# V projected with x as the stationary operand, and a plain fp32 beginning by halves, in a two-layer attention trunk on one core

## The chip, the cores and the metric

The kernel runs on one core of one Trainium2 chip. The metric is the device time of one execution in microseconds (us). The kernel before has a median of 774.34 us over 3 runs (774.07 to 775.7).

A core has a matrix engine (TensorE, PE in the profile; its weight loads are PEld), a vector engine (VectorE, DVE), an activation engine (ScalarE, ACT), a general engine (GpSimd, POOL) and SyncE (SP), which here issues nearly all transfers from memory. The engines run apart and wait for each other by semaphores.

## What is computed

The reference is a trunk of two layers on x of 256 tokens by 1024 columns, fp32. Layer A uses stick-breaking attention, layer B dilated window attention; both are followed by a SwiGLU. The change touches only the first part of layer A, which is this (cut to what matters):

```python
def rms_norm(x, g):
    y = xf * lax.rsqrt(jnp.mean(xf * xf, axis=-1, keepdims=True) + RMS_EPS)
    return (y * g).astype(x.dtype)

def mixer_a(xn, w_qkv, w_o):
    qkv = (xn @ w_qkv).reshape(b, s, 3, N_HEADS, HEAD_DIM)      # 16 heads of 64
    o = stick_breaking_attention(q, k, v)
    return o.reshape(b, s, D_MODEL) @ w_o

# stick_breaking_attention, strict: s < t
z = einsum('qd,kd->qk', q, k) * scale
log_stay = where(strict, log_sigmoid(-z), 0.0)
log_a = log_sigmoid(z) + cumsum(after, reverse=True)
a = where(strict, exp(log_a), 0.0)
out = einsum('qk,kd->qd', a, v)
```

## The kernel before, in words

**Products in high and low parts.** Weights and activations are cut into a high part (fp32r) and a low part, the rest. A product is three matmuls: high by high, high by low, low by high. Weights come in units: SyncE loads a unit into one of 3 places of `raw`, ScalarE makes the high part (`hi`, L476), VectorE the low part (`lo`, L758), each into one of 6 places. In layer A a unit is 128 x 1024 (1024 rows by 128 columns of q, k or v: one pair of heads); from the output weights on it is 128 x 2048. A place of `raw` is free again when its unit's low part is made, and SyncE waits for that before it loads (L306).

**Layer A.** The 16 heads go in 8 pairs. For pair p TensorE projects q, k and v (`project_a`, 24 matmuls each of 256 moving columns: the weights are the stationary operand, x the moving one). The result stands with columns on partitions, which is right for q and k, but V has to be turned: VectorE copies it out with the norm's row factor (`take_v_a`, L886), TensorE turns it by two transposes (`turn_v`, L1214), ScalarE copies it to `va` (L552).

The order of TensorE in a step p: scores of pair p-1 (L1205, L1206), outputs of pair p-2 (L1238, L1240), turning of pair p-1, q, k and the first 6 matmuls of v of pair p, the running sums of pair p-1 (L1227), the other 18 of v. Between scores and sums lies this chain: ScalarE takes absolute value, exponential and logarithm (L544, L546, L548), VectorE makes the softplus and its mask (L858, L860), `arg` (L861), ScalarE the high part (L554), VectorE the low part (L863). After the sums VectorE subtracts them (`stay_a`, L870), ScalarE takes the exponential (L557), VectorE masks (L875). In between stand the cuts of the units of weights. The order of every engine is written out by hand.

**After the last pair** come the output product (`out_proj`, L1150 to L1152, in slices k of the 1024 rows, 512 moving columns) mixed with the last outputs and sums, then the boundary to the SwiGLU.

**The beginning.** SyncE loads the unit matrix `eye`, x in two tiles of 128 tokens (512 KB each), the first query weights by halves, the key and value weights of pair 0, and small things. TensorE runs some matmuls on zeros (`keep_busy`), turns x (16 transposes), and projects. ScalarE and VectorE make the high and low parts of the turned x with its gain (`cut_both`) and of the first two units by halves.

## Time and profile before

| | |
|---|---|
| median of 3 runs | 774.34 us |
| the profiled execution | 774.78 us |
| its span, from first to last instruction | 772.9 us |
| TensorE busy | 763.6 us, 99% |
| VectorE busy | 506.8 us, 66% |
| ScalarE busy | 398.8 us, 52% |
| transfers | 139.17 MB, mean 180 GB/s |

Times inside the program are microseconds from the start of the span. Matmuls overlap, so the distance between the starts of two rows says more than the duration of one. Plain fp32 matmuls are recorded as two passes each. In the timeline, a bracket at the end tells how long the engine was idle before and whom it waited for.

### The profile page before, as it was taken

The page shows a single profiled execution, that of the slowest core. Times are in us where ns is not written, and L with a number is a line of the kernel's source. Part 1 is how long each engine was busy: PE and PEld are TensorE (multiplying, and loading weights), DVE is VectorE, ACT ScalarE, POOL GpSimd, SP SyncE. Part 2 cuts the span into 40 slices and gives each one's busy share as a digit, 9 for nine tenths or more (in the row PEclk, how much of TensorE's full clock was granted, in tenths as well). Part 3 has the DMA queues.
Part 4 walks back from the last instruction along what each step waited for, and adds up shares of the span by engine and source line. Part 5 has one row for each costly group of instructions (what it writes and reads, how often), then busy time and mean ns, then how long its engine had stood idle before and what let it go on. Part 6 is the DMA issues. An engine that isn't in the chain of part 4 may idle for free.

```text
span 772.9 us, 12842 instructions
## 1 busy us (share of the span) xinstructions
PE 763.6 (99%) x4533; PEld 657.7 (85%) x4533; DVE 506.8 (66%) x688; ACT 398.8 (52%) x542; POOL 113.6 (15%) x173
## 2 busy tenths in 40 slices
PE   8999999999999999999999999999999999999996
PEld 7999987878888888999898898898888888888885
DVE  6788987766545545868768668567647755554543
ACT  5665676454334344756666566656545534433421
POOL 2000001520000000215225235144002000000000
PEclk9999999999999999999999999999999999999999
DMA  7534866686665454569775685685643856556502
GB/s 232 163 114 141 234 214 226 199 240 218 204 210 183 163 189 137 145 158 220 189 214 147 164 224 142 163 234 178 215 136 92 290 193 199 179 188 215 193 0 54
DMA packets 161538, 139.17 MB, mean 180 GB/s; under 512 B 6617, under 2 KB 151105, under 8 KB 161505
## 3 DMA queue, kind: packets, MB, share of 16 engines
q1 hardware_dynamic: 157536, 131.55, 55.2%
q0 software_dynamic: 3712, 6.88, 4.9%
q8 instruction: 20, 0.33, 0.2%
q10 hardware_dynamic: 256, 0.30, 0.1%
q14 instruction: 14, 0.11, 0.0%
HBM read 137.60 MB, written 1.11 MB: 179 GB/s over the span
## 4 chain that ended last, share of the span: by engine, by line
PE 93%; DMA 2%; DVE 2%; ACT 1%; issue 1%; SPq 0%; DVEq 0%; POOLq 0%; POOL 0%; ACTq 0%
PE ps L1150 19%; PE ps L1152 19%; PE ps L1151 19%; PE ps L1384 10%; PE ps L1386 5%; PE ps L1156 4%; PE ps L1157 4%; PE ps L1158 4%; DMA raw<-in_w_gate_up 2%; PE ps L1442 1%; DVE w_lo L758 1%; PE ps L1298 1%; PE ps L1412 1%; PE ps L1451 1%; PE ps L1227 1%; ACT w_hi L476 1%
## 5 line engine op out<-in xcount | busy, mean ns | idle before, releaser
L758 DVE TENSOR_TENSOR w_lo<-raw,w_hi 128x2048 fp32r<-128x2048 f32 (+2 forms) x144 | 279.2, 1954 | 48.4 <-ACT w_hi L476 47.1
L476 ACT ACTIVATE w_hi<-raw 128x2048 fp32r<-128x2048 f32 (+2 forms) x144 | 232.7, 1637 | 60.6 <-DMA raw<-in_w_kv_b 22.9
L1150 PE MATMUL ps<-w_hi,xt 128*128 128x512 f32 x352 | 139.5, 396 | 0.0
L1152 PE MATMUL ps<-w_hi,xt 128*128 128x512 f32 x352 | 137.3, 390 | 0.0
L1151 PE MATMUL ps<-w_lo,xt 128*128 128x512 f32 x352 | 137.1, 389 | 0.0
L637 ACT ACTIVATE work<-ps,stat 128x256 f32<-128x256 f32 x44 | 20.9, 476 | 191.8 <-PE ps L1152 191.8
L1150 PE MATMUL ps<-w_hi,ot 128*128 128x512 f32 x240 | 95.0, 396 | 0.7 <-DVE ot L1011 0.4
L1152 PE MATMUL ps<-w_hi,ot 128*128 128x512 f32 x240 | 93.5, 390 | 0.0
L1151 PE MATMUL ps<-w_lo,ot 128*128 128x512 f32 x240 | 93.5, 390 | 0.0
L1152 PEld LDWEIGHTS ps<-w_hi,xt 128*128 128x128 f32 x352 | 66.1, 188 | 14.0
L1150 PEld LDWEIGHTS ps<-w_hi,xt 128*128 128x128 f32 x352 | 66.1, 188 | 13.6 <-issue 0.6
L1151 PEld LDWEIGHTS ps<-w_lo,xt 128*128 128x128 f32 x352 | 66.2, 188 | 12.8
L1009 DVE CAST ot<-ps 128x512 fp32r<-128x512 f32 x22 | 15.2, 691 | 75.5 <-PE ps L1298 75.5
L389 POOL TENSOR_SCALAR stat<-stat 128x1 f32<-128x1 f32 x16 | 10.3, 644 | 366.1 <-ACT work L492 343.2
L1156 PE MATMUL ps<-xt,w_hi 128*128 128x256 f32 x216 | 62.0, 287 | 0.8 <-DVE w_lo L1050 0.8
L1157 PE MATMUL ps<-xt,w_hi 128*128 128x256 f32 x216 | 61.1, 283 | 0.0
L1158 PE MATMUL ps<-xt,w_lo 128*128 128x256 f32 x216 | 61.0, 283 | 0.0
L1150 PEld LDWEIGHTS ps<-w_hi,ot 128*128 128x128 f32 x240 | 45.1, 188 | 11.1 <-DVE w_lo L758 1.0
L1152 PEld LDWEIGHTS ps<-w_hi,ot 128*128 128x128 f32 x240 | 45.0, 188 | 9.6
L1151 PEld LDWEIGHTS ps<-w_lo,ot 128*128 128x128 f32 x240 | 45.1, 188 | 8.9
L429 POOL TENSOR_TENSOR work<-mask_b,work 128x512 f32<-128x512 bf16 x16 | 24.6, 1537 | 137.4 <-DVE stat L939 95.7
L1156 PEld LDWEIGHTS ps<-xt,w_hi 128*128 128x128 f32 x216 | 41.3, 191 | 2.2 <-DVE w_lo L1050 1.4
(143 smaller groups left out, 1211.9 us busy)
## 6 DMA issues: line engine op xcount, KB each, us to landing
raw<-in_w_gate_up SPq DMA_DIRECT2D x88, 512.0 KB, 4.8
raw<-in_w_kv_b SPq DMA_DIRECT2D x96, 256.0 KB, 3.9
raw<-in_w_down SPq DMA_DIRECT2D x22, 1024.0 KB, 4.9
raw<-in_w_q_b SPq DMA_DIRECT2D x48, 256.0 KB, 4.0
raw<-in_w_qkv_a SPq DMA_DIRECT2D x23, 512.0 KB, 4.7
raw<-in_w_o_a SPq DMA_DIRECT2D x4, 1024.0 KB, 7.4
work<-bias_rows POOLq DMA_DIRECT2D x64, 64.0 KB, 3.7
raw<-in_w_o_b SPq DMA_DIRECT2D x4, 1024.0 KB, 6.0
```

The lines of the kernel that those rows point to most:

```text
L429: pool.tensor_tensor(ends[0], ends[1], turned_band, ALU.add)
L476: act.activation(w_hi[:, s % CUT, 0:size(s)], raw[:, s % RAW, 0:size(s)], ACT.Copy).then_inc(hi_made, 1)
L637: act.activation(silu[:, t, :], bank(4 + t, 0, FC), ACT.Silu, scale=x_rs(2 * l + 1, t)).then_inc(silu_made, 1)
L758: dve.tensor_tensor(w_lo[:, c, 0:n], raw[:, s % RAW, 0:n], w_hi[:, c, 0:n].bitcast(F32), ALU.subtract).then_inc(lo_made, 1)
L1150: mm(out, xs[0], ws[0], start=start, stop=False)
L1151: mm(out, xs[0], ws[1], start=False, stop=False)
L1152: return mm(out, xs[1], ws[0], start=False, stop=stop)
L1156: mm(out, ws[0], xs[0], start=start, stop=False)
L1157: mm(out, ws[0], xs[1], start=False, stop=False)
L1158: return mm(out, ws[1], xs[0], start=False, stop=stop)
L1384: mm(both, w[k // 4][0][:, k % 4, g, :], x_[:, :, k, :], start=k == 0, stop=False, skip_group_check=True)
L1386: inst = mm(bank(b, 0, SEQ), w[k // 4][1][:, k % 4, g, :], x_[:, 0, k, :], start=False, stop=k == KT - 1, skip_group_check=True)
```

## The change

**V.** The x is now the stationary operand and the weights the moving one. The result has tokens on partitions, as the outputs need it; no V copy on VectorE and no transposes. One V unit is half of the 1024 rows by 256 columns, that is two pairs of heads; units 2h and 2h+1 give V for pairs 2h and 2h+1. `values_a(h)` has 24 matmuls of 256 columns. Units of pair 0 and 1 come in the beginning, and step p projects V unit p+1 behind the sums, so the last step has none. ScalarE copies both pairs' V to `va` with the row factor, at every second pair.

**The beginning.** x and the first query weights are loaded by halves in turn: the first 512 columns of both token tiles, the first half of the query weights, then the second halves. Each half is turned, copied with its gain to `xf` (plain fp32, ScalarE and VectorE one bank each), and multiplied by the plain fp32 weights, without cuts, 8 matmuls for q and 8 for k. The high and low parts of x are made from `xf` for what follows. The diagonal of row factors is made by VectorE and no more by GpSimd. `eye` is loaded from ScalarE's queue. Because the first q and k need no cut units, the units' numbers shift by two (`A0 = -2`). The mask is loaded after step 1, and x is loaded a second time behind the output weights.

```diff
-A0 = 0
+A0 = -2
...
+        def query_a(p):
+            return A0 + (3 * p + 1 if p else 0)
+        def value_a(h):
+            return A0 + (3 * h if h else 2)
...
+                elif s >= 1:
+                    sp.wait_ge(first_used, s)
...
-            sp.dma_start(eye[:, :], square[:, 0, :]).then_inc(eye_in, 16)
-            for t in range(NT):
-                sp.dma_start(xn[:, t, :], x_dram[t]).then_inc(x_in[t], 16)
-            first = raw[:, 0, 0:KT * P].rearrange("p (k n) -> p k n", k=KT)
-            sp.dma_start(first[:, 0:4], qkv_dram[:, 0, 0:4, 0:P]).then_inc(first_in, 16)
-            sp.dma_start(first[:, 4:8], qkv_dram[:, 0, 4:8, 0:P]).then_inc(landed[0], 16)
-            pair_a(0, 0, (1, 2))
+            for half in range(2):
+                k4, cols = slice(4 * half, 4 * half + 4), slice(HALF * half, HALF * half + HALF)
+                for t in range(NT):
+                    sp.dma_start(xn[:, t, cols], x_dram[t][:, cols]).then_inc(x_in[t][half], 16)
+                sp.dma_start(first_w[0][:, k4], qkv_dram[:, 0, k4, 0:P]).then_inc(first_in[half], 16)
+            sp.dma_start(first_w[1], qkv_dram[:, 1, :, 0:P]).then_inc(first_in[2], 16)
+            half_values_a(0, 0)
...
+            half_values_a(1, 0)
+            step_a(1, 0)
             sp.dma_start(mask_in, mask).then_inc(mask_in_s, 16)
...
+            query_key_a(PAIRS - 1, 0)
+            for u in range(4):
+                two_rows(WOA0 + u, 0, wo_dram[0][:, 2 * u:2 * u + 2, :])
             sp.wait_ge(xt_done, 4)
             sp.wait_ge(xsq_made, NT)
             for r in range(R):
                 sp.dma_start(xn[RUN * (r % 2):RUN * (r % 2) + RUN, r // 2, :], by_residue(x[0])[r]).then_inc(x_again, 16)
...
-                act.wait_ge(vt_done, j * 2 + a + 1)
-                if a >= 1:
-                    act.wait_ge(pva_done, j * 2 + a)
-                act.activation(va, bank(2, 0, SEQ), ACT.Copy).then_inc(va_made, 1)
+                if a % 2 == 0:
+                    act.wait_ge(w_used, j * 6 + value_a(a + 1) + 1)
+                    act.wait_ge(*((pva_done, j * 2 + a) if a else (xrs_made, NT)))
+                    for t in range(NT):
+                        inst = act.activation(va[:, t, :], bank(2, 2 * P * t, 2 * P), ACT.Copy, scale=x_rs(0, t))
+                    inst.then_inc(va_made, 1)
...
+            for half in range(2):
+                turned_x(2 * half)
+                act.wait_ge(xf_act, half + 1)
+                act.wait_ge(xf_dve, half + 1)
+                ks = slice(4 * half, 4 * half + 4)
+                act.activation(xt[:, 0, ks, :], xf[:, ks, :], ACT.Copy).then_inc(xt_hi, 4 * NT)
...
             dve.wait_ge(gain_made, 1)
...
+            turned_x(1)
+            square_first(0)
+            square_first(1)
+            turned_x(3)
...
+            def first_columns(c, ks=range(KT)):
+                for k in ks:
+                    if c == 0:
+                        if k % 2 == 0:
+                            pe.wait_ge(xf_dve if k % 4 else xf_act, k // 4 + 1)
+                        if k % 4 == 0:
+                            pe.wait_ge(first_in[k // 4], 16)
+                    elif k == 0:
+                        pe.wait_ge(first_in[2], 16)
+                    inst = mm(bank(0, SEQ * c, SEQ), first_w[c][:, k, :], xf[:, k, :], start=k == 0, stop=k == KT - 1)
...
-            def turn_v(a, j):
...
+            def values_a(h, j, ks=range(4)):
+                s, half = value_a(h), h % 2
+                pe.wait_ge(lo_made, j * 6 + s + 1)
...
+                w = cut_unit(s, k=4)
+                for k in ks:
+                    for t in range(NT):
+                        out, xs = bank(2, 2 * P * t, 2 * P), [xt[:, n, 4 * half + k, P * t:P * t + P] for n in range(2)]
+                        mm(out, xs[0], w[0][:, k, :], start=not half and k == 0 and t == 0, stop=False,
+                           skip_group_check=True)
+                        mm(out, xs[0], w[1][:, k, :], start=False, stop=False, skip_group_check=True)
+                        inst = mm(out, xs[1], w[0][:, k, :], start=False, stop=half == 1 and k == 3, skip_group_check=True)
...
-                turn_v(p - 1, j)
                 project_a(p, j, 0, 0, 0)
                 project_a(p, j, 1, 0, SEQ)
-                project_a(p, j, 2, 1, 0, range(2))
                 sums_a(p - 1, j)
-                project_a(p, j, 2, 1, 0, range(2, KT))
+                values_a(p + 1, j)
...
-            keep_busy(5)
+            keep_busy(3)
...
+            for half in range(2):
+                ks = range(4 * half, 4 * half + 4)
+                for t in range(NT):
+                    pe.wait_ge(x_in[t][half], 16)
+                    for k in ks:
+                        inst = pe.transpose(bank(4 + k // 2, SEQ * (k % 2) + P * t, P), xn[:, t, P * k:P * k + P],
+                                            eye[:, :])
...
+                keep_busy(1)
+                first_columns(0, ks)
+            first_columns(1)
             pe.wait_ge(ones_in, 16)
             spread_rows(1)
...
+            values_a(0, 0)
+            values_a(1, 0)
```

TensorE at the very beginning, before: L1487 is the matmul on zeros, L1498 the transposes of x, L1156 to L1158 the three matmuls of a product.

```order
1 L1487 MATMUL ps<-rows 128x256 [waits zeros_made]
2 L1487 MATMUL ps<-rows 128x256 x4
3 L1494 MATMUL ps<-eye,work 128x72 [waits gain_in,eye_in]
4 L1498 MATMUL ps<-eye,xn 128x128 [waits x_in0]
5 L1498 MATMUL ps<-eye,xn 128x128 x7
6 L1498 MATMUL ps<-eye,xn 128x128 [waits x_in1]
7 L1498 MATMUL ps<-eye,xn 128x128 x7
8 L1487 MATMUL ps<-rows 128x256 x4
9 L1156 MATMUL ps<-xt,w_hi 128x256 [waits xt_made,first_lo]
```

TensorE at the same place in the changed kernel: L1509 is the matmul on zeros, L1522 a transpose of x, L1207 a plain fp32 matmul of the first q and k.

```order
2 L1509 MATMUL ps<-rows 128x256 x2
3 L1516 MATMUL ps<-eye,work 128x72 [waits gain_in,eye_in]
4 L1522 MATMUL ps<-eye,xn 128x128 [waits x_in00]
6 L1522 MATMUL ps<-eye,xn 128x128 [waits x_in10]
8 L1509 MATMUL ps<-rows 128x256
9 L1207 MATMUL ps<-work,raw 128x256 [waits first_in0,xf_act]
11 L1207 MATMUL ps<-work,raw 128x256 [waits xf_dve]
13 L1522 MATMUL ps<-eye,xn 128x128 [waits x_in01]
17 L1509 MATMUL ps<-rows 128x256
18 L1207 MATMUL ps<-work,raw 128x256 [waits first_in1,xf_act]
20 L1207 MATMUL ps<-work,raw 128x256 [waits xf_dve]
22 L1207 MATMUL ps<-work,raw 128x256 [waits first_in2]
```

The second half's transposes stand behind the first four products, and four of the nine matmuls on zeros are gone.

VectorE in the last two pairs, before: L858 to L863 are the softplus chain of pair 6, L879 and L880 take q and k of pair 7, L886 takes V, L870 subtracts the sums, L758 makes the low part of a unit.

```order
106 L863 TENSOR_TENSOR xkv<-work,xkv 128x768 [waits spl_hi]
107 L879 SCALAR_TENSOR_TENSOR work<-ps,rows 128x256 [waits w_used]
108 L880 TENSOR_TENSOR work<-ps,rows 128x256
109 L758 TENSOR_TENSOR w_lo<-raw,w_hi 128x2048 [waits hi_made]
110 L886 TENSOR_TENSOR work<-ps,rows 128x256 [waits vt_done,w_used]
111 L870 TENSOR_TENSOR work<-work,ps 128x2x256 [waits r_done,arg_made]
113 L758 TENSOR_TENSOR w_lo<-raw,w_hi 128x2048 [waits hi_made]
114 L875 TENSOR_TENSOR work<-work 128x2x2x128 [waits wts_made]
115 L858 SCALAR_TENSOR_TENSOR work<-ps,work 128x768 [waits ell_made]
```

VectorE at the same place in the changed kernel: L872 to L877 are the softplus chain, L893 and L894 take q and k, L884 subtracts the sums, L772 makes the low part.

```order
88 L772 TENSOR_TENSOR w_lo<-raw,w_hi 128x1024 [waits hi_made]
89 L772 TENSOR_TENSOR w_lo<-raw,w_hi 128x2048 [waits hi_made]
90 L854 CAST ot<-ps 128x256 [waits pva_done]
92 L872 SCALAR_TENSOR_TENSOR work<-ps,work 128x768 [waits ell_made]
95 L877 TENSOR_TENSOR xkv<-work,xkv 128x768 [waits spl_hi]
96 L893 SCALAR_TENSOR_TENSOR work<-ps,rows 128x256 [waits w_used]
97 L894 TENSOR_TENSOR work<-ps,rows 128x256
98 L884 TENSOR_TENSOR work<-work,ps 128x2x256 [waits r_done,arg_made]
100 L772 TENSOR_TENSOR w_lo<-raw,w_hi 128x2048 [waits hi_made]
101 L889 TENSOR_TENSOR work<-work 128x2x2x128 [waits wts_made]
102 L872 SCALAR_TENSOR_TENSOR work<-ps,work 128x768 [waits ell_made]
```

The first cut of 2048 columns has moved ahead of the softplus chain of pair 6, and the V copy is gone.

## Rows read from the trace of the kernel before

**Rows 1.** The page's busy table: busy us, share of the span, instructions.

```profile
PE 763.6 (99%) x4533; PEld 657.7 (85%) x4533; DVE 506.8 (66%) x688; ACT 398.8 (52%) x542; POOL 113.6 (15%) x173
```

**Rows 2.** Timeline, TensorE's beginning: start us, duration us, engine, line, operation.

```profile
1.31 2.50 PE L1487 MATMUL ps<-rows 128*128 128x256 f32 x5 [1.31 <-DVE rows L1039]
...
5.57 2.06 PE L1498 MATMUL ps<-eye,xn 128*128 128x128 f32 x16
...
7.47 1.89 PE L1487 MATMUL ps<-rows 128*128 128x256 f32 x8
...
9.60 0.39 PE L1156 MATMUL ps<-xt,w_hi 128*128 128x256 f32 x1 [0.24 <-DVE w_lo L1050]
...
16.78 1.03 PE L1508 MATMUL ps<-work 32*16 32x512 f32 x2
...
20.80 0.71 PE L1205 MATMUL ps<-work 64*128 64x256 f32 x4
```

**Rows 3.** Timeline, the beginning on the other engines and SyncE's queue.

```profile
2.27 0.44 SPq L348 DMA_DIRECT2D raw<-in_w_qkv_a  x1
...
5.14 1.23 DVE L1057 CUSTOM_DVE_ANT_0 work<-xn 128x1024 f32<-128x1024 f32 x1 [3.88 <-DMA xn<-in_x]
...
6.53 1.22 DVE L1057 CUSTOM_DVE_ANT_0 work<-xn 128x1024 f32<-128x1024 f32 x1 [0.15 <-DMA xn<-in_x]
...
7.10 0.84 ACT L670 ACTIVATE xt<-ps,gains 128x256 fp32r<-128x256 f32 x2 [1.10 <-PE ps L1498]
...
12.85 1.06 ACT L476 ACTIVATE w_hi<-raw 128x1024 fp32r<-128x1024 f32 x1 [0.41 <-DMA raw<-in_w_qkv_a]
```

**Rows 4.** Line L348, the first query weights: from issue to landing.

```profile
DMA to landing us min/median/max: 5.8/5.8/5.8
```

**Rows 5.** Busy time by windows; behind the engines the granted clock, DMA share, GB/s.

```profile
0.00:5.00 5.00, 3.69 (x9) 2.97 (x10) 0.27 (x1) 1.28 (x1) 0.29 (x5) 1.00 0.55 193
```

**Rows 6.** Timeline, TensorE in steady attention steps.

```profile
43.26 0.71 PE L1205 MATMUL ps<-work 64*128 64x256 f32 x4
...
51.73 1.10 PE L1227 MATMUL ps<-xkv 128*128 128x512 f32 x6
52.67 0.28 PE L1156 MATMUL ps<-xt,w_hi 128*128 128x256 f32 x1
...
54.91 0.71 PE L1205 MATMUL ps<-work 64*128 64x256 f32 x4
...
56.65 0.44 PE L1214 MATMUL ps<-eye,work 128*128 128x128 f32 x2
...
57.04 0.28 PE L1157 MATMUL ps<-xt,w_hi 128*128 128x256 f32 x1
```

**Rows 7.** Timeline, VectorE in the first and in a steady step.

```profile
27.05 0.96 DVE L863 TENSOR_TENSOR xkv<-work,xkv 128x768 fp32r<-128x768 f32 x1
...
42.22 1.22 DVE L758 TENSOR_TENSOR w_lo<-raw,w_hi 128x1024 fp32r<-128x1024 f32 x1
...
50.06 0.96 DVE L863 TENSOR_TENSOR xkv<-work,xkv 128x768 fp32r<-128x768 f32 x1
```

**Rows 8.** Timeline, the last two pairs and the output product, three engines.

```profile
86.70 1.10 PE L1227 MATMUL ps<-xkv 128*128 128x512 f32 x6
...
108.88 3.71 ACT L476 ACTIVATE w_hi<-raw 128x2048 fp32r<-128x2048 f32 x2
...
109.01 0.96 DVE L863 TENSOR_TENSOR xkv<-work,xkv 128x768 fp32r<-128x768 f32 x1 [0.36 <-ACT xkv L554]
...
110.82 2.29 DVE L758 TENSOR_TENSOR w_lo<-raw,w_hi 128x2048 fp32r<-128x2048 f32 x1
...
111.93 1.08 PE L1227 MATMUL ps<-xkv 128*128 128x512 f32 x6
...
116.39 0.50 PE L1150 MATMUL ps<-w_hi,ot 128*128 128x512 f32 x1 [0.18 <-DVE w_lo L758]
```

**Rows 9.** Busy time by windows: length; PE, PEld, DVE, ACT, POOL; clock, DMA.

```profile
86.70:116.39 29.69, 29.37 (x194) 25.11 (x192) 26.65 (x33) 19.61 (x20) 0.00 (x0) 1.00 0.75 231
```

More of the change, by code:

```diff
@@ L171, in build @@
         squares_a = carve(D, at)
+        xf = carve(KT * SEQ).rearrange("p (k s) -> p k s", k=KT)
+        first_w = [raw[:, 1 + c, 0:KT * P].rearrange("p (k n) -> p k n", k=KT) for c in range(2)]
         post = carve(D, 0)
@@ L833, in take_rows @@
                 dve.wait_ge(rows_done, use)
[L834 removed]
+                dve.tensor_copy(rows[:, :], bank(use, 0, SEQ)).then_inc(rows_made, 1)
                 dve.wait_ge(rows_made, use)
@@ L1059, in _ @@
             dve.wait_ge(gain_made, 1)
-            cut_both(0)
-            lo_half(0, 0)
-            cut_both(1)
-            cut_both(2)
-            lo_half(0, 1)
-            cut_both(3)
-            lo_half(1, 0)
-            lo_half(1, 1)
+            turned_x(1)
+            square_first(0)
+            square_first(1)
+            turned_x(3)
+            for half in range(2):
+                dve.wait_ge(xt_hi, 4 * NT * (half + 1))
+                ks = slice(4 * half, 4 * half + 4)
+                dve.tensor_tensor(xt[:, 1, ks, :], xf[:, ks, :], xt[:, 0, ks, :].bitcast(F32), ALU.subtract
+                                  ).then_inc(xt_made, 4 * NT)
+            dve.wait_ge(eye_in, 16)
+            make_diagonal(0)
+            lo(A0 + 2)
             take_rows(1)
-            lo(A0 + 2)
             take_qk_a(0, 0)
@@ L1207, in scores_a @@
                 inst.then_inc(z_done, 1)
-            def turn_v(a, j):
-                pe.wait_ge(vat_made, j * 2 + a + 1)
-                if a >= 1:
-                    pe.wait_ge(va_made, j * 2 + a)
-                for t in range(NT):
-                    inst = pe.transpose(bank(2, P * t, P), va_t[:, P * t:P * t + P], eye[:, :])
-                inst.then_inc(vt_done, 1)
+            def values_a(h, j, ks=range(4)):
+                s, half = value_a(h), h % 2
+                pe.wait_ge(lo_made, j * 6 + s + 1)
+                if h == 0:
+                    pe.wait_ge(xt_made, KT * NT)
+                elif not half:
+                    pe.wait_ge(va_made, j + h // 2)
+                w = cut_unit(s, k=4)
[6 more added lines that the diff above has]
+                        inst = mm(out, xs[1], w[0][:, k, :], start=False, stop=half == 1 and k == 3, skip_group_check=True)
+                if k == 3:
+                    inst.then_inc(w_used, 1)
             def sums_a(a, j):
@@ L1494, in _ @@
             pe.transpose(bank(3, 0, 9 * KT), gain_in[0:9 * KT, :], eye[0:9 * KT, 0:9 * KT]).then_inc(gain_done, 1)
[L1495 to L1502 removed]
+            for half in range(2):
+                ks = range(4 * half, 4 * half + 4)
[4 more added lines that the diff above has]
+                                            eye[:, :])
+                        if t and k % 2:
+                            inst.then_inc(xt_done, 1)
+                keep_busy(1)
+                first_columns(0, ks)
+            first_columns(1)
             pe.wait_ge(ones_in, 16)
             spread_rows(1)
[L1505 removed]
             pe.wait_ge(bias_in, 32)
```

137 lines of the change are left out of this document (47 added, 90 removed).

## The prediction

> **What bounds the kernel now.** I read the page's busy table first, then the timeline of the first 30 us, of one attention step and of the passage from attention to the output product, and the busy time by windows. The reader is to see that TensorE is busy 99% of the span [rows 1]: outside the opening almost nothing else stands in the sum, so a change counts by the matmul time it takes out of TensorE's row, and by the waits it makes or removes there.
>
> In the opening TensorE works on nothing useful until 9.60 us [rows 2]: x lands at 5.14 and 6.53 [rows 3], is turned and copied with its gain, the first half of the query weights lands at 2.27 + 5.8 = 8.07 [rows 3, 4], and the cuts into high and low parts follow. The first scores of attention start at 20.80 [rows 2]; I call this S. In a steady step scores start at 43.26 and again at 54.91: 11.65 us, without a gap [rows 6]. In the last stretch, from the sums of pair 5 (86.70) to the seventh slice of the output product (116.39), 29.69 us pass, in which VectorE is busy 26.65 [rows 8, 9]: nearly as full as TensorE.
>
> **Part 1: turning V round.** It removes eight times two transposes. In the step at 54.91 they stand at 56.65, and the second matmul behind them starts at 57.04, where one spacing (0.12) before it would be 56.92: 56.92 - 56.65 = 0.27 us [rows 6]. The matmuls of V are as many as before (24 of 256 columns a step, 0.12 apart: 18 of them fill 52.67 to 54.91 [rows 6]); only the operands change sides, and moving columns, which set the spacing, stay 256. I cost that at zero. VectorE loses one copy of 0.42 a step; ScalarE copies 512 columns every second step for 256 every step, under idle time.
>
> The sums now come right behind K, 6 matmuls of V (0.72) and the turning (0.27) sooner after the scores. What is late next: the cut of the softplus (L863). In the opening step it ends at 27.05 + 0.96 = 28.01, 7.21 after S [rows 7]; TensorE arrives 0.9 (scores) + 0.05 + 48 x 0.12 = 6.7 after S. So the first step gets a wait of 0.6: sums at S + 7.3, where before has its sums at S + 7.6, six V matmuls and the turning later than 6.7. In steady steps the value products stand between: 1.74 for scores and outputs (54.91 to 56.65) + 5.8 = 7.55 after the scores, against 50.06 + 0.96 - 43.26 = 7.76 for the cut in before, which falls to about 7.25 because VectorE no longer makes the V copy ahead of it [rows 6, 7]. Slack 0.3: a step costs 11.65 - 0.27 = 11.38. The second step, with its table load on ScalarE, I take at 11.55. From S to the sums of pair 5 this gives 7.3 + 11.55 + 4 x 11.38 = 64.4, against 86.70 - 20.80 = 65.9: **minus 1.5**. Bounds: minus 1.9 (no wait) and plus 0.5 (the cut 0.3 late in every step).
>
> **Part 2: the last two steps.** Between the sums of pairs 5 and 7 TensorE loses 18 V matmuls (2.15) and two turnings (0.54): sums of pair 7 could stand at 111.93 - 86.70 - 2.7 = 22.5 [rows 8]. But VectorE keeps its work there, less 2 x 0.42, and the cut of the first output-weight unit (2.29 instead of about 1.2 for a small one, [rows 8] and [rows 7]) moves one step ahead, onto the path of pair 6: its softplus cut ends at about 11.65 after the sums of pair 5, and sums of pair 6 start at 11.75 instead of 11.4. Scores of pair 7 at 12.7. ScalarE then has two cuts of output weights (3.71, [rows 8]) from 10.6 to 14.3, and the exponential of pair 6 to 15.1, which holds up pair 7's chain by 1.4: L863 of pair 7 ends at 12.7 + 7.21 + 1.4 = 21.3, starts at 20.35. From there before shows 109.01 to 110.82 until the third output unit's cut and 110.82 to 116.39 until the waiting matmul, VectorE without a pause [rows 8]: 1.81 + 5.57, so 27.7. TensorE alone, its sums of pair 7 at 22.9 after the late start, would be there at 22.9 + 4.46 - 0.2 (its wait in before) = 27.2. Result 27.6 against 29.69: **minus 2.1**. Bounds: minus 3.0 (TensorE alone, nothing late) and 0 (VectorE's chain as long as now). Output weights are asked for earlier, since the mask and the second loading of x leave their place ahead of them; they land before ScalarE is free, so this is worth nothing by itself. Where the second loading of x goes, behind the last output unit, its user is some 10 us away.
>
> **Part 3: the beginning.** Work on TensorE before S: in before 72 matmuls of 256 columns for q, k, v of pair 0 (8.6). In after 16 plain fp32 matmuls for q and k and 48 for V of pairs 0 and 1. An fp32 matmul of 256 columns is two passes; eight passes take 1.89 [rows 2], 0.47 with the tail, so 0.45 each: 16 x 0.45 = 7.2, plus 48 x 0.12 = 5.75: 12.95, 4.3 more. (One V unit more is done by S; part 1 has counted that as the order of the steady steps.)
>
> What comes sooner: SyncE's first issue is x, not the unit matrix, 0.47 earlier; x comes by quarters of 256 KB. x as a whole took 6.53 - 5.14 = 1.39 for 512 KB, so a quarter 0.7: the first two at about 3.9 and 4.6, the first half of the weights (8.07 - 6.53 = 1.5 for 256 KB in short packets) at 6.0, the other quarters 6.7 and 7.4, weights 8.8, key weights 10.7, V unit 12.2 (12.85 in before, [rows 3]). Eight transposes end at 5.5, the busy matmul at 5.9, the gain copies (two of 0.42, [rows 3]) at 6.15 and 6.5: query product from 6.2, 3.4 sooner than 9.60. Four matmuls to 8.0; transposes of the second half to 8.9; copies to 9.75; four matmuls 9.8 to 11.6; eight for k to 15.1; row sums 0.5 and the bias product 1.03 [rows 2] to 16.7; V 2 x 2.9 to 22.4. S at 22.5 against 20.80: **plus 1.7**. VectorE has the two sums of squares (1.23 each, [rows 3]) at 6.7 to 9.5, ahead of its second pair of copies, which then end at 10.5; they are wanted at 10.7, the third matmul of that half. The V units' cuts are due at 16.7 and 19.5 and done at 14.5 and 18.2: the second is asked for at 11.6, when the query matmuls free its place. Key and query weights of pair 1 follow at 15.2 and 15.7 behind it and are cut by 21.8 and 23, wanted at 23.4 and 26.3. Bounds: plus 0.3 (quarters 0.7 sooner, second half's copies not waited for) and plus 4.5 (below).
>
> **The clock in the opening.** Five passes of the first fp32 matmuls take 2.50 us, 0.50 each, against 0.24 for those at 7.47, the pace of 1.2 against 2.4 GHz, though the granted clock of the first 5 us is printed as 1.00 [rows 2, 5]. Before keeps TensorE on such matmuls up to 5.5; after has three of them, ending near 3.9, and then transposes. The Trainium skill, "TensorE: Matmul & The Clock Gate", Part 4 (PE-mode transpose), says that transposes do not count as activity for the clock; by that the first half would still run at the low pace. The trace of before shows 16 transposes in 2.06 us at the high one [rows 2], but only behind the matmuls, so it cannot decide. The Trainium skill, "DMA: Bandwidth & Descriptors", section on the anatomy of one DMA, gives about 2.0 us fixed per transfer; by that the first quarter could be there at 0.86 + 2.0 + 0.65 = 3.5, 0.4 before my figure, without effect on the sum, since the weights land last.
>
> **Sum.** 1.7 - 1.5 - 2.1 = -1.9 us. The profiled execution took 774.78 us (span 772.9), 0.44 above the median of 774.34. Behind the seventh slice everything is unchanged and TensorE-bound, so 1.9 passes through whole: 774.34 - 1.9 = **772.4**.
>
> **Rivals.**
> Slow clock (slower than before). Place: TensorE from 3.9 to about 10, when it has idled between three busy matmuls and the first transposes. Price: eight transposes 0.9, one busy matmul 0.45 and four query matmuls 4 x 0.45 = 1.8 more, half hidden by waiting for weights at the front, and the second half's transposes 0.9: S later by 2.5 to 3. It decides as soon as the low pace lasts beyond 8 us. Time 772.4 + 2.8 = 775.2. For it: the missing busy matmuls. Against it: the gap is short. Chance 0.15.
> VectorE binds (no change). For it: 26.65 busy of 29.69, and slack of only 0.3 in each step. If the cut is 0.2 late in each of six steps (1.2) and the last stretch gives 1.5 instead of 2.1: 774.2. Against it: VectorE loses over 0.4 us a step. Chance 0.2.
> The opening goes better (faster by more). If x's second half is turned and copied without TensorE waiting and fp32 spacing is 0.43: S at 21.2, time 771.0. For it: 9.2 to 9.8 is the only wait I count. Against it: the copies depend on transposes that come after the first four products. Chance 0.17.
> That the change doesn't do what it says (V still turned somewhere): the program's order has no transposes of V left. Chance 0.
> The forecast itself: 0.48.
>
> **How the numbers follow.** Two runs of this kernel differ by about 0.2% or 1.55 us; faster means under 772.8, slower over 775.9. The forecast's own spread, 771.5 to 773.5, lies two thirds under 772.8: 0.33 of 0.48, and with the good opening 0.17: faster 0.50. Same takes the rest of the forecast (0.15), nearly all of VectorE-binds (0.19) and part of the slow clock, which only beyond 775.9 counts as slower: I give slower 0.12 (with the open ends of the bounds, both parts late together), same 0.38. Range 770.5 to 775.4.
>
> **What would show it.** In the profile of after: query matmuls from about 6.2; S at 22.5; first sums 7.3 behind S with a wait of 0.6 on VectorE; steps of 11.38; last stretch 27.6, with a wait on the cut of output weights of up to 1 us at the fifth slice of the output product. The prediction is wrong if S is beyond 24, if passes of the query product stand 0.43 apart, or if steady steps are still 11.65.

## The result, and the profile after

The changed kernel takes 776.56 us (median of 11 runs, 775.25 to 777.79); the kernel before, on the same chip, 774.55. The ratio is 1.0027 with a 95% interval of 1.0019 to 1.0034: slower by 2.0 us, where 1.9 us less was forecast, and outside the range. A profile shows one execution: that of after is 0.7 above its median, so small differences between two profiles can be scatter. The profiled execution of after took 777.25 (span 775.5), that of before 774.78 (span 772.9).

First the page's busy table of after, against [rows 1]: 40 TensorE instructions and 12 of VectorE fewer, one microsecond less busy on TensorE, and yet a span 2.6 longer. The time went into waits.

```profile
PE 762.6 (98%) x4493; PEld 655.3 (84%) x4493; DVE 504.4 (65%) x676; ACT 397.7 (51%) x536; POOL 113.4 (15%) x171
```

The waits of TensorE name the places at once (engine, line, what it waited for, us in total, times, longest). First before, then after.

```profile
PE ps L1487 <- DVE rows L1039: 1.3, 1, 1.3
PE ps L1156 <- DVE w_lo L1050: 0.8, 2, 0.5
PE ps L1150 <- DVE ot L1011: 0.4, 1, 0.4
PE ps L1150 <- DVE w_lo L758: 0.2, 1, 0.2
```

```profile
PE ps L1516 <- DMA work<-in_g_kv: 3.0, 1, 3.0
PE ps L1250 <- DVE xkv L877: 1.5, 1, 1.5
PE ps L1509 <- DVE rows L1046: 1.3, 1, 1.3
PE ps L1154 <- DVE w_lo L772: 0.4, 1, 0.4
```

Two are new and large: 3.0 us on the gain rows ahead of the first transposes (L1516), and 1.5 us ahead of the first sums (L1250), which the forecast had as 0.6.

The timeline of TensorE in after, from the start to the output product (start, duration, engine and line, operation, count, idle time before it and what ended it), answers to [rows 2, 6 and 8]:

```profile
1.31 2.93 PE L1509 MATMUL ps<-rows 128*128 128x256 f32 x6 [1.31 <-DVE rows L1046]
7.21 0.25 PE L1516 MATMUL ps<-eye,work 72*128 72x72 f32 x1 [2.98 <-DMA work<-in_g_kv]
7.30 1.52 PE L1522 MATMUL ps<-eye,xn 128*128 128x128 f32 x8
...
9.47 2.75 PE L1207 MATMUL ps<-work,raw 128*128 128x256 f32 x8
12.06 1.04 PE L1522 MATMUL ps<-eye,xn 128*128 128x128 f32 x8
...
13.81 5.45 PE L1207 MATMUL ps<-work,raw 128*128 128x256 f32 x24 [0.28 <-ACT work L691]
...
26.53 0.71 PE L1217 MATMUL ps<-work 64*128 64x256 f32 x4
34.85 1.20 PE L1250 MATMUL ps<-xkv 128*128 128x512 f32 x6 [1.45 <-DVE xkv L877]
...
69.46 1.10 PE L1250 MATMUL ps<-xkv 128*128 128x512 f32 x6
80.87 1.10 PE L1250 MATMUL ps<-xkv 128*128 128x512 f32 x6
...
119.71 0.50 PE L1154 MATMUL ps<-w_hi,ot 128*128 128x512 f32 x1 [0.41 <-DVE w_lo L772]
```

The reader is to see three things. The query product (L1207) starts at 9.47, no sooner than in before (9.60). Eight fp32 passes take 2.75 at 9.47, but 24 take 5.45 at 13.81. And a step is 80.87 - 69.46 = 11.41, where before has 11.65 [rows 6]. Before's marks stand beside these so:

| | before | predicted | after |
|---|---|---|---|
| scores of pair 0 start (S) | 20.80 | 22.5 | 26.53 |
| S to the first sums | 7.6 | 7.3 | 8.32 |
| S to the sums of pair 5 (at 92.28 in after) | 65.9 | 64.4 | 65.75 |
| a steady step | 11.65 | 11.38 | 11.41 |
| from there to the seventh slice of the output product | 29.69 | 27.6 | 27.43 |
| rest of the span behind it | 656.5 | the same | 655.8 |

The window of the last stretch in after (us; busy time of PE, PEld, DVE, ACT, POOL; granted clock; DMA share; GB/s), against [rows 9]:

```profile
92.28:119.71 27.43, 26.99 (x172) 22.58 (x170) 25.27 (x31) 18.93 (x19) 0.00 (x0) 1.00 0.71 222
```

So the seventh slice starts 3.3 us later than in before (119.71 against 116.39), and the rest gives 0.7 back. That 0.7 isn't the work of V: all twelve of the experiments' profiles below have it too (655.8 to 656.0 behind that slice), also the one with V the old way. Before waits 0.4 once for L1011, far behind the opening, and after does not; I take that to be part of it, but no run singled it out.

Where the opening went: the DMA issues of SyncE and ScalarE in after.

```profile
0.86 0.89 SPq L368 DMA_DIRECT2D xn<-in_x  x2
1.79 0.43 SPq L369 DMA_DIRECT2D raw<-in_w_qkv_a  x1
2.27 0.98 SPq L368 DMA_DIRECT2D xn<-in_x  x2
...
0.86 0.42 ACTq L682 DMA_DIRECT2D eye<-in_square  x1
1.32 0.53 ACTq L683 DMA_DIRECT2D work<-in_norm_gains  x1
1.88 0.73 ACTq L684 DMA_DIRECT2D work<-in_g_kv  x1
```

The unit matrix (L682, 64 KB) lands 3.8 us after its issue, at 4.7; in before, at the front of SyncE's queue, it took 1.9. Behind it on ScalarE's queue the last gain rows (4 KB) are asked for at 1.88 and let TensorE go only at 7.21. x comes no sooner either: its quarters land 3.6, 4.4, 5.7 and 5.9 after their issues, the last at 8.7, where x was complete at 6.53 in before [rows 3]. The windows of after (columns as above) show what the engines moved meanwhile:

```profile
2.00:2.50 0.50, 0.50 (x3) 0.41 (x2) 0.00 (x0) 0.00 (x0) 0.00 (x0) 1.00 0.77 158
3.50:4.00 0.50, 0.50 (x2) 0.01 (x1) 0.00 (x0) 0.43 (x1) 0.00 (x0) 1.00 1.00 230
4.00:4.50 0.50, 0.24 (x1) 0.00 (x0) 0.00 (x0) 0.00 (x0) 0.00 (x0) 1.00 0.69 211
4.50:5.00 0.50, 0.00 (x0) 0.00 (x0) 0.00 (x0) 0.00 (x0) 0.00 (x0) 1.00 0.81 208
```

Before moves 217 GB/s in the first of these half microseconds, and 386, 350 and 435 in the last three. The second of its four rows:

```profile
3.50:4.00 0.50, 0.50 (x2) 0.35 (x2) 0.00 (x0) 0.00 (x1) 0.00 (x0) 1.00 0.98 386
```

TensorE also ran at its low pace for a while. Taken one by one, the first four transposes behind the wait start 0.11 apart (7.30 to 7.63), but from 7.76 on they start 0.21 apart, and the zero passes and the first four query passes 0.42 to 0.51 apart; from 11.20 on the query passes start 0.22 apart again. The granted clock of the windows says the same, 1.00 up to 7.5, 0.50 from 8.0 to 11.0, and 1.00 from 11.5:

```profile
8.00:8.50 0.50, 0.50 (x4) 0.50 (x3) 0.00 (x0) 0.00 (x1) 0.00 (x0) 0.50 1.18 307
11.50:12.00 0.50, 0.50 (x4) 0.44 (x3) 0.50 (x1) 0.00 (x0) 0.50 (x1) 1.00 0.63 147
```

### The profile page after: what moved, and what is told of

Read it like the earlier page. It is cut to its first block, busy times and chain, and to the rows that moved or that the text cites. A ratio compares the mean times of both kernels' runs of the same rounds, so it can differ in the third digit from the quotient of the medians.

```text
span 775.5 us, 12710 instructions
## 1 busy us (share of the span) xinstructions
PE 762.6 (98%) x4493; PEld 655.3 (84%) x4493; DVE 504.4 (65%) x676; ACT 397.7 (51%) x536; POOL 113.4 (15%) x171
## 4 chain that ended last, share of the span: by engine, by line
PE 96%; DMA 1%; DVE 1%; ACT 1%; issue 0%; ACTq 0%; DVEq 0%; POOLq 0%; POOL 0%
PE ps L1154 20%; PE ps L1156 20%; PE ps L1155 20%; PE ps L1406 10%; PE ps L1408 5%; PE ps L1160 2%; PE ps L1162 2%; PE ps L1161 2%; PE ps L1464 1%; PE ps L1320 1%; PE ps L1434 1%; PE ps L1250 1%; PE ps L1473 1%; PE ps L1207 1%; PE ps L1235 1%; PE ps L1233 1%
## 5 line engine op out<-in xcount | busy, mean ns | idle before, releaser
L772 DVE TENSOR_TENSOR w_lo<-raw,w_hi 128x2048 fp32r<-128x2048 f32 (+2 forms) x144 | 280.1, 1961 | 48.9 <-ACT w_hi L494 47.3
L1156 PE MATMUL ps<-w_hi,xt 128*128 128x512 f32 x352 | 137.3, 390 | 0.0
L1156 PE MATMUL ps<-w_hi,ot 128*128 128x512 f32 x240 | 93.5, 390 | 0.0
L1156 PEld LDWEIGHTS ps<-w_hi,xt 128*128 128x128 f32 x352 | 66.1, 188 | 14.0
L1156 PEld LDWEIGHTS ps<-w_hi,ot 128*128 128x128 f32 x240 | 45.1, 188 | 9.6
L1009 DVE SCALAR_TENSOR_TENSOR work<-ps,stat,work 128x256 f32<-128x256 f32 x44 | 21.1, 479 | 34.1 <-ACT work L657 34.1
L1406 PE MATMUL ps<-xkv,w_hi 128*128 128x512 f32 x168 | 43.2, 399 | 0.0
L1154 PE MATMUL ps<-w_hi,xkv 128*128 128x384 f32 x128 | 43.1, 337 | 0.0
L1156 PE MATMUL ps<-w_hi,xkv 128*128 128x384 f32 x128 | 42.8, 335 | 0.0
```

The source lines that it names most:

```text
L772: dve.tensor_tensor(w_lo[:, c, 0:n], raw[:, s % RAW, 0:n], w_hi[:, c, 0:n].bitcast(F32), ALU.subtract).then_inc(lo_made, 1)
L1009: dve.scalar_tensor_tensor(hid[:, t, :], bank(4 + t, FC, FC), x_rs(2 * l + 1, t), silu[:, t, :], ALU.mult, ALU.mult).then_inc(hid_made, 1)
L1154: mm(out, xs[0], ws[0], start=start, stop=False)
L1156: return mm(out, xs[1], ws[0], start=False, stop=stop)
L1406: mm(both, w[k // 4][0][:, k % 4, g, :], x_[:, :, k, :], start=k == 0, stop=False, skip_group_check=True)
```

## The experiments

The kernel before beside them took 774.53 (the first four here), 774.67 (the unit matrix moved, five zero matmuls, the unit cut later, everything together) and 774.44 (the other four). k7 below is the start of the seventh slice of the output product (116.39 in before, 119.71 in after).

### Which half of the change costs

**V turned round alone**, with the beginning of before (diff shortened, the words behind # are not in the code):

```diff
-A0 = -2
+A0 = 0
...
-            for half in range(2):                      # x and query weights by halves, fp32 products
+            sp.dma_start(eye[:, :], square[:, 0, :])   # as before: x by tiles, everything cut
+            for t in range(NT):
+                sp.dma_start(xn[:, t, :], x_dram[t])
```

> V turned round as in the change, with the beginning of the kernel before (x by whole tiles, cut units, gain rows first on ScalarE's queue). Theory A (the loss lies in the opening alone: gain rows that land late, and the slow pace after it): the steps keep the gain measured in the changed kernel (11.41 us a step, 27.4 us in the last stretch), so about 0.8 us faster than before, 773.7, with no slow stretch at the front. Theory B (V turned round costs as much as it saves, because the sums wait for the softplus cut): 774.5 or more.

Measured 774.0, ratio 0.9992 (0.9983 to 1.0001). Scores start at 23.84, since two V units now stand ahead of them for one. TensorE's waits in it:

```profile
PE ps L1252 <- DVE xkv L886: 1.4, 1, 1.4
PE ps L1511 <- DVE rows L1055: 1.3, 1, 1.3
...
PE ps L1164 <- DVE w_lo L781: 0.4, 1, 0.4
```

The first step has the same wait for the softplus cut as after (1.4), though the opening is the old one: that wait comes with V and the order of loads that goes with it. From S to k7 it takes 93.18, to the hundredth what after takes (119.71 - 26.53); before takes 95.59. The interval just includes no change, so the gain of 0.5 isn't shown beyond doubt.

**The fp32 beginning alone**, V the old way (against the kernel before, shortened):

```diff
+            for half in range(2):                      # after's beginning
+                for t in range(NT):
+                    sp.dma_start(xn[:, t, cols], x_dram[t][:, cols])
+                sp.dma_start(first_w[0][:, k4], qkv_dram[:, 0, k4, 0:P])
...
+            pair_a(0, 0, (2,))                         # V of pair 0 as before, turned by L1216
```

> The fp32 beginning of the change (halves, unit matrix on ScalarE's queue ahead of the gain rows) with V turned the old way. Theory A: the first transpose of the gain rows waits until about 7.2 us as in the changed kernel, scores of the first step start near 23.7 against 20.8; 2.9 to 3.5 us slower than before, 777.4 to 778. Theory B (the loss comes with V): within 1 us of before.

Measured 777.92, ratio 1.0045 (1.0032 to 1.0059): slower by 3.4. Of the two parts only this one costs. The time is as expected, its parts are not: the gain rows let TensorE go at 6.05 and not at 7.2, though they are asked for in the same order as in after, and S is at 22.68, 1.9 behind before. Another 1.3 is lost between S and k7, nearly all of it in a second new wait, where V is turned while the softplus is under way:

```profile
6.05 0.35 PE L1496 MATMUL ps<-eye,work 72*128 72x72 f32 x1 [1.80 <-DMA work<-in_g_kv]
...
24.83 0.44 PE L1216 MATMUL ps<-eye,work 128*128 128x128 f32 x2 [1.22 <-DVE work L879]
```

### What in the opening costs

**Gain rows asked for ahead of the unit matrix**, on the same queue:

```diff
-            act.dma_start(eye[:, :], square[:, 0, :]).then_inc(eye_in, 16)
             act.dma_start(gain_in[0:8 * KT, :], gain_rows).then_inc(gain_in_s, 16)
             act.dma_start(gain_in[8 * KT:9 * KT, :], ...).then_inc(gain_in_s, 16)
+            act.dma_start(eye[:, :], square[:, 0, :]).then_inc(eye_in, 16)
```

> The changed kernel with one thing moved: on ScalarE's queue the two loads of gain rows stand ahead of the unit matrix. Theory A1 (it is the queue place of the gain rows): they land 0.4 us or more earlier than 7.2, but the unit matrix is now last in that queue and may take its place as the last to land; the gain is 0.4 to 1.5 us against the changed kernel, 775 to 776. Theory A2 (small rows crawl behind x whatever their place in their queue): no difference, 776.5.

Measured 777.26, ratio 1.0035 (1.0023 to 1.0046), no better than after. The wait changed its name and kept most of its length:

```profile
6.91 0.38 PE L1516 MATMUL ps<-eye,work 72*128 72x72 f32 x1 [2.67 <-DMA eye<-in_square]
```

So neither transfer is the slow one, and of the expectations the second came true. Whichever is last on ScalarE's queue, beside x on SyncE's, is late.

**TensorE kept busy through the wait**: nine zero matmuls at the front for three.

```diff
-            keep_busy(3)
+            keep_busy(9)
```

> The changed kernel with nine instead of three matmuls on zeros at the front: TensorE is then busy until about 7, where it idled for 3 us. Theory A, clock part: eight transposes, one matmul on zeros and four query matmuls run at full pace, so the second half starts 1.0 to 1.3 us earlier and the time is 775.3. Rival: the low pace there costs nothing, since the copies and the weights are late too: 776.5.

Measured 776.62, ratio 1.0027 (1.0016 to 1.0037), the time of after.

```profile
1.32 7.00 PE L1509 MATMUL ps<-rows 128*128 128x256 f32 x18 [1.32 <-DVE rows L1046]
8.15 0.23 PE L1516 MATMUL ps<-eye,work 72*128 72x72 f32 x1
8.22 1.04 PE L1522 MATMUL ps<-eye,xn 128*128 128x128 f32 x8
...
10.03 1.99 PE L1207 MATMUL ps<-work,raw 128*128 128x256 f32 x8 [0.34 <-ACT work L691]
11.86 1.04 PE L1522 MATMUL ps<-eye,xn 128*128 128x128 f32 x8
```

Kept busy, TensorE does the same transposes in 1.04 instead of 1.52 and the same query passes in 1.99 instead of 2.75; from the gain rows' transpose to those of the second half it takes 11.86 - 8.15 = 3.71, where after takes 12.06 - 7.21 = 4.85. The low pace of after's opening is worth 1.1 us. But the zero matmuls themselves hold TensorE until 8.15, 0.9 later than the gain rows let it go in after, so the sum is nearly the same. The rival's time came true, but not its reason.

**The unit matrix at the front of SyncE's queue**, its place in before:

```diff
+            sp.dma_start(eye[:, :], square[:, 0, :]).then_inc(eye_in, 16)
             for half in range(2):
...
-            act.dma_start(eye[:, :], square[:, 0, :]).then_inc(eye_in, 16)
```

> The changed kernel with the unit matrix back at the front of SyncE's queue, gain rows alone on ScalarE's. Theory A (the late small loads hold TensorE's in-order queue): both small loads land by about 5.3 us as in the kernel before, x a queue place (0.45 us) later; the transpose of the gain rows starts near 5.0 to 5.5 instead of 7.2, and with it everything: 1.5 to 2 us faster than the changed kernel, near 774.8. Rival (it is the x quarters and their weights that hold the front; the small loads only look like the cause): less than 0.5 us of difference, 776.3.

Measured 774.93, ratio 1.0006 (0.9997 to 1.0015).

```profile
4.80 0.35 PE L1516 MATMUL ps<-eye,work 72*128 72x72 f32 x1 [0.56 <-DMA work<-in_g_kv]
...
5.99 0.66 PE L1522 MATMUL ps<-eye,xn 128*128 128x128 f32 x4 [0.38 <-DMA xn<-in_x]
...
7.42 1.99 PE L1207 MATMUL ps<-work,raw 128*128 128x256 f32 x8 [0.34 <-ACT work L691]
...
23.72 0.71 PE L1217 MATMUL ps<-work 64*128 64x256 f32 x4
32.46 1.21 PE L1250 MATMUL ps<-xkv 128*128 128x512 f32 x6 [1.87 <-DVE xkv L877]
```

One line moved takes out nearly the whole loss, as expected: k7 at 117.36, 2.35 sooner than in after, and 1.6 us in the time. The wait of 2.98 is down to 0.56, the transposes of x and the query passes run at the high pace, and x's quarters land 3.5 to 4.8 after their issue instead of 3.6 to 5.9, although they are asked for 0.47 later. Of the 2.81 won at S, 0.42 goes again into the first step's wait (1.87 for 1.45).

**The same with five zero matmuls**, to close the rest of the idle time:

```diff
-            keep_busy(3)
+            keep_busy(5)
```

> As e5_eye_sync, and five instead of three matmuls on zeros at the front. If the low pace costs what e4_busy9 showed (4.85 us against 3.71 from the first gain transpose to the second half's first x transpose), another 0.8 to 1.1 us: near 773.8. Rival: with the small loads early, copies and weights bind and the pace is hidden: no difference from e5_eye_sync.

Measured 774.98, ratio 1.0006: no difference. The gain rows are turned at 5.74 for 4.80, and S stands at 24.54 for 23.72. In this profile TensorE works without a pause from 1.31, and still the first transposes start 0.21 apart, up to 6.93; only then is the spacing 0.11. The version with everything together (below) does the same work up to there, and has that spacing from 5.45 on. Their eight transposes, first here, then there:

```profile
5.86 1.61 PE L1522 MATMUL ps<-eye,xn 128*128 128x128 f32 x8
...
5.45 1.12 PE L1526 MATMUL ps<-eye,xn 128*128 128x128 f32 x8
```

So how long the low pace of the opening lasts differs from one profile to the next, and idle time alone doesn't explain it.

**x ahead of the query weights**, instead of by turns, on top of the unit matrix first:

```diff
             for half in range(2):
                 for t in range(NT):
                     sp.dma_start(xn[:, t, cols], x_dram[t][:, cols])
+            for half in range(2):
                 sp.dma_start(first_w[0][:, k4], qkv_dram[:, 0, k4, 0:P])
```

> e5_eye_sync with the four quarters of x ahead of the two halves of the query weights instead of in turn with them. Theory (taking turns costs, since the transfers share the same bandwidth): x is complete near 6.5 us as in the kernel before, where it lands at 8.1 in e5_eye_sync; but the first query product must wait for its weights. Time within 0.5 us of e5_eye_sync, 774.9, faster at most by 0.5. Rival (turns are what the beginning needs): first product later by 1 us and the time 775.9.

Measured 776.5, ratio 1.0033 (1.002 to 1.0046). The rival is right in the time. The query product waits for its weights and starts at 8.08 for 7.42; in this profile its first passes also run at the low pace (starts 0.42 to 0.56 apart up to 9.49), which makes the other half of the 1.33 by which S is later (25.05 for 23.72). What the order alone costs is therefore not shown.

```profile
8.08 2.67 PE L1209 MATMUL ps<-work,raw 128*128 128x256 f32 x8 [0.34 <-DMA raw<-in_w_qkv_a]
```

### What the first step waits for

In after the V unit of pairs 2 and 3 is cut on ScalarE at 27.62, when the scores (ready at 27.46) should have been taken:

```profile
27.62 1.06 ACT L494 ACTIVATE w_hi<-raw 128x1024 fp32r<-128x1024 f32 x1 [1.42 <-DMA raw<-in_w_qkv_a]
28.59 0.80 ACT L562 ACTIVATE work<-ps 128x768 f32<-128x768 f32 x1
```

**That unit cut later**, behind the first softplus, in the kernel with V alone:

```diff
-            for u in range(2, 7):
+            for u in range(2, 6):
                 hi(A0 + u)
...
+                attend_a(a, j, [...], (lambda: hi(s - 1, j)) if a == 0 else None)
...
+                if p == 1:
+                    lo(s - 1, j)
                 take_qk_a(p, j)
```

> e1_v_only (V turned round, old beginning) with one unit moved: the cut of the V unit of pairs 2 and 3 stands behind the first softplus on ScalarE and VectorE instead of in front of it. Theory: in e1_v_only ScalarE takes up the first scores 1.1 us late because it waits for that unit to land, and TensorE then waits 1.4 us for the cut softplus; with the move the wait falls to 0.3 to 0.6 and the time by about 0.8 us, to 773.2. Rival: the wait comes back at the V unit's own cut or in the second step: no difference from 774.0.

Measured 775.65, ratio 1.0012 (1.0003 to 1.0021), 1.6 above V alone. The wait of the first step went, and came back in the second. The two together are only 0.3 longer than the 1.39 of V alone, and k7 is 0.5 later, so most of the 1.6 isn't explained:

```profile
31.21 1.20 PE L1256 MATMUL ps<-xkv 128*128 128x512 f32 x6 [0.40 <-DVE xkv L889]
44.36 1.20 PE L1256 MATMUL ps<-xkv 128*128 128x512 f32 x6 [1.27 <-DVE xkv L889]
```

**Everything together** (after, the unit matrix first, five zero matmuls, the unit cut later: the diffs above):

> The changed kernel with all three: unit matrix at the front of SyncE's queue, five matmuls on zeros, the V unit's cut behind the first softplus. Sum of the parts: 1.7 + 0.9 + 0.9 below 776.6, so near 773.1; that would beat the kernel before and e1_v_only. Rival: the fp32 products (7.2 against 5.7 us on TensorE) eat what the halves save, and it is not below e7_v_only_late_unit.

Measured 775.23, ratio 1.0009 (0.9999 to 1.0018). The waits are the same pair, 0.40 and 1.32, and it is no better than with the unit matrix moved alone: the three parts don't add up.

**The mask loaded later**, so that this V unit isn't loaded beside it (V alone). Before loads the mask behind the weights of the last pair, so this takes back a move of the change:

```diff
             step_a(1, 0)
-            sp.dma_start(mask_in, mask).then_inc(mask_in_s, 16)
             step_a(2, 0)
...
                 two_rows(WOA0 + u, 0, wo_dram[0][:, 2 * u:2 * u + 2, :])
+            sp.dma_start(mask_in, mask).then_inc(mask_in_s, 16)
```

> e1_v_only (V turned round, old beginning) with one load moved: the mask (384 KB), which the change asks for after step 1, is loaded behind the output weights. Theory: in e1_v_only the V unit of pairs 2 and 3 is asked for at about 19.0 us and lands at 24.9, with the mask asked for at 19.4 beside it; without the mask it lands about 1 us sooner and TensorE's first wait for the cut softplus (1.4 us) falls by 0.6 to 1.0: time 773.3. Rival: the unit's place in the queue and not the mask sets its landing: 774.0.

Measured 773.81, ratio 0.9991 (0.9983 to 1.0). The cut on ScalarE, first with V alone and then with the mask late as well:

```profile
24.89 1.06 ACT L497 ACTIVATE w_hi<-raw 128x1024 fp32r<-128x1024 f32 x1 [2.87 <-DMA raw<-in_w_qkv_a]
```

```profile
23.28 1.06 ACT L497 ACTIVATE w_hi<-raw 128x1024 fp32r<-128x1024 f32 x1 [1.18 <-DMA raw<-in_w_qkv_a]
```

The unit is there 1.6 sooner, ScalarE is free when the scores come, and the wait for the softplus cut falls from 1.39 to 0.40: the prediction had 0.6. k7 stands at 115.82 for 117.02. In the median only 0.2 of these 1.2 us is to be seen, within the spread of the runs: the profile with the mask late is of the fastest of its eleven runs (773.38), that of V alone of the second slowest (774.55), and 0.2 of the 1.2 lies ahead of S. That the shorter wait is worth its 1.0 us in the time is not shown.

**The mask later, and the low part of the second V unit made before q and k are taken** (V alone):

```diff
             lo(A0 + 2)
-            take_qk_a(0, 0)
             lo(A0 + 3)
+            take_qk_a(0, 0)
```

> As e9_v_only_mask_late, and VectorE makes the low part of the second V unit before it takes the first q and k, so that the next unit is asked for about 1 us sooner. Theory: together the wait of the first step falls to 0.4 or less, 773.0, and the kernel beats the one before and e1_v_only. Rival: the wait comes back in the second step, as in e7_v_only_late_unit: 773.5 to 774.

Measured 773.65, ratio 0.9988 (0.9979 to 0.9997). The unit is cut at 22.64, but k7 (115.91) and the time are those of the run before. It is the best version of all, 0.8 us below the kernel before and the only one whose interval lies below no change, if barely, and 2.9 below after.

**The mask later in the full change**, with the unit matrix first:

```diff
+            sp.dma_start(eye[:, :], square[:, 0, :]).then_inc(eye_in, 16)
...
             step_a(1, 0)
-            sp.dma_start(mask_in, mask).then_inc(mask_in_s, 16)
...
                 two_rows(WOA0 + u, 0, wo_dram[0][:, 2 * u:2 * u + 2, :])
+            sp.dma_start(mask_in, mask).then_inc(mask_in_s, 16)
```

> e5_eye_sync (the whole change, unit matrix at the front) with the mask's load moved behind the output weights as in e9_v_only_mask_late. Theory: the same 0.6 to 1.0 us come out of the first wait (1.9 us here): 774.1. Rival (here the unit waits for the fp32 key product to free its place and not for bandwidth): 774.9.

Measured 774.55, ratio 1.001 (1.0001 to 1.0019). The median is 0.1 above the kernel before, but the runs fall into two groups: six from 774.25 to 774.55 and five from 775.7 to 776.55, which is why the ratio says 1.001. The profile is of the lower group. It has k7 at 116.58, and the wait of the first step at 1.32, 0.55 less than with the mask early: the V unit lands at 24.46 for 25.21. With V alone it lands at 23.26, though it is asked for only 0.34 sooner. Here two other loads go out together, at 16.26 and 16.68, when the key product has ended, and run ahead of it. That they make the rest of the wait is read from these rows; no run took them away.

## Why the prediction was wrong

The forecast had k7 at 116.39 - 1.9 = 114.5; it stands at 119.7, 5.2 later: 4.0 ahead of S, 1.35 in the steps, and 0.2 won back in the last stretch. Behind the seventh slice, where the forecast had nothing change, 0.7 came back. By its own steps:

**The beginning (forecast plus 1.7, measured plus 5.7).** This is the step that failed, and in it the words "SyncE's first issue is x, not the unit matrix, 0.47 earlier" and "query product from 6.2". The 0.47 was booked as a gain, and the other end of the move left out: the matrix and the gain rows, now on ScalarE's queue beside x, are wanted by the first transposes. They let them start at 7.21 instead of about 4.4 (the eight were to end at 5.5). The query product started at 9.47 (forecast 6.2), and by the second half's transposes the lateness was 12.06 - 8.0 = 4.06. Behind that point the working held: the row sums that follow k start at 19.09, 4.0 after the forecast 15.1, and S is 26.53 - 22.5 = 4.03 late. With the matrix moved back S is 2.8 sooner and the time 1.6 us shorter, so the cause is shown for 2.8 of the 4.03. The other 1.2 stays (23.72 for 22.5): there the query product starts at 7.42, not at 6.2, because the second quarter of x lands at 5.9, not at 4.6. So even without the slip this term was plus 2.9 and not plus 1.7.

**The quarters of x** were sized as half of x's 1.39, that is by a rate measured when the stream was under way. They landed at 4.5, 5.7, 8.0 and 8.7 for 3.9, 4.6, 6.7 and 7.4. With the matrix in front they landed at 4.9, 5.9, 7.4 and 8.1, and TensorE waited 0.38 for the second. The Trainium skill, "DMA: Bandwidth & Descriptors", section on the anatomy of one DMA, gives its 2.0 us for transfers that GpSimd issues. By it the prediction had the first quarter at 3.5; SyncE's first quarter landed at 4.5 in after and at 4.0 to 4.9 with the matrix in front.

**The clock.** "Wrong if passes of the query product stand 0.43 apart": the first four did. The first rival's picture held in part: TensorE was idle between its zero matmuls and the transposes, and ran at the low pace from 7.76 to 11.20. But the first four transposes behind the idle time ran at the high pace, and its price was 2.5 to 3 in the forecast and 1.1 measured; the idle time itself (2.98) cost more than the pace. The rival's time of 775.2 is nearer than the forecast, with its place right and its main cause missing.

**fp32 passes** were sized right: 24 of them in 5.45, 0.22 apart, 0.44 to 0.45 a matmul.

**V turned round, the steps (forecast minus 1.5, measured minus 0.15).** The steady step is 11.41 against 11.38, so this sign of being wrong did not come. The first step is the miss: 8.32 for 7.3. The forecast had the softplus cut 7.21 behind the scores as in before, and did not see that ScalarE now cuts one V unit more there, which is loaded beside the mask. The change had moved the mask up, and the forecast priced only the place that this left free. With V alone, the later load of the mask brought the wait from 1.39 to 0.40 in the profile, and in the full change from 1.87 to 1.32. The other 0.3 lies in the next two steps (11.68 and 11.51).

**The last two steps (forecast minus 2.1, measured minus 2.26).** Right, and by its mechanism: 27.43 for 27.6, the sums of pair 6 start 11.61 behind those of pair 5 (forecast 11.75), those of pair 7 22.97 (22.9), VectorE is busy 25.27. Only the wait on the output weights' cut, 0.41, stands at the seventh slice and not at the fifth.

**The parts as a sum.** The forecast contains 24 more V matmuls ahead of S (2.9), so that V alone was worth 2.9 - 1.5 - 2.1 = -0.7 and the fp32 beginning 1.7 - 2.9 = -1.2. Measured: V alone -0.5, the beginning on top of it +2.6 (776.56 - 774.0). V's -0.5 isn't a clean hit either: at k7 it was 0.63 behind before, and the 0.7 of the rest made it good.

**What the beginning is worth when repaired.** With the matrix in front S is at 23.72, with the old beginning at 23.84: 16 fp32 matmuls (7.2) take the place of 48 of 0.12 (5.8), and starting the query product 2.4 sooner (7.42 for 9.84) pays for that, and for the transposes of the second half and the copies behind them, which now stand in the middle of the product (9.25 to 10.99), and for no more. The time is 774.93 against 774.0.

## What to carry to other kernels

When a small load is moved off the front of a queue to make room for a large one, ask who needs it first, and count it as landing behind what it now runs beside; a few KB that everything waits for go first. A step worth 0.3 us in steady state can be hidden by one unit that lands late in the first, so each first step is to be worked out for itself. And a change of several parts is judged by its parts: here one gained 0.5 us at most, not clear of the scatter, and the other lost 2.6.

## What the runs showed of the hardware

- A small load doesn't pass a large one on another queue. The unit matrix (64 KB) took 1.9 us from issue to landing ahead of x and 3.8 beside it; the last gain rows (4 KB, asked for at 1.88) let TensorE go at 7.21 beside matrix and x, in another profile with the same order at 6.05, and at 4.80 with the matrix on the other queue, where they are asked for 0.42 sooner. The Trainium skill, "DMA: Bandwidth & Descriptors", section on queues, rings and completion order, says that each DMA engine goes round its queues a packet at a time; the trace agrees in that ScalarE's loads are neither first nor shut out, but shows delays of several us, which its rule does not give.
- DMA engines that are marked busy may move little: 230, 211 and 208 GB/s in after from 3.5 to 5.0, against 386, 350 and 435 in before; from 3.5 to 4.0 at a share of 1.00 and 0.98. What slows them there no run separated.
- TensorE can lose its pace in the opening after it had it. In after it was idle from 4.2 to 7.2, ran four transposes 0.11 apart, and only then fell to the low pace, at a granted clock of 0.50 from 8.0 to 11.0; it rose again while TensorE was busy. An idle time of 0.56 was not followed by such a fall. Eight fp32 passes took 1.99 at the high pace and 2.75 where the first four ran at the low one.
- How long the first low pace lasts is not a matter of the kernel's idle time alone. Without a pause from 1.31 on, it lasted to about 5.2 in before and with everything together, and to 7.0 with the unit matrix first and five zero matmuls, where it ended between transposes. With a pause it lasted to 9.6 with x first (idle for 0.48) and to 5.8 with the mask later (0.49). The printed granted clock is 1.00 all this time, though fp32 passes start 0.43 apart, so in an opening the spacing is the better sign.
- Versions with three zero matmuls at the front scatter more: 775.25 to 777.79 for after and 775.74 to 778.8 with x first, and the two groups of the last experiment lie 1.7 apart. Those with five lie closer: 773.63 to 774.73 for V alone, 774.37 to 775.55 and 774.63 to 775.91 with the fp32 beginning (unit matrix first, and everything together). But the kernel before, with five too, spreads from 773.68 to 776.57 over 29 runs. That the scatter is the pace of the opening would fit this, but it wasn't tried.
